# Band stage of layer 0: scores issued two units ahead and next to the values, with minima and exponentials reordered to match

## What is computed

```python
s = jnp.einsum('bcqhd,bckhd->bchqk', qc, kb).astype(F32) * (HD_A ** -0.5)
s = s + rel_bias_lookup(table, dist)
p = jax.nn.softmax(s, axis=-1).astype(v.dtype)
o = jnp.einsum('bchqk,bckhd->bcqhd', p, vb)
...
y = jnp.concatenate([mix_o, cross_attn(xq, mk, mv)], axis=-1) * jax.nn.silu(gate)
return x + y @ w
```

## Time and profile before

| what | value |
|---|---|
| median of 3 runs | 2691.19 us (2688.42 to 2704.43) |
| span of the profiled execution | 2696.0 us |
| TensorE busy | 2554.8 us, 95% |
| VectorE busy | 1918.9 us, 71% |
| ScalarE busy | 1457.8 us, 54% |
| GpSimd busy | 353.8 us, 13% |
| band stage in the trace | about 700 to 1415 us |

### The profile page before, as it was taken

How to read it: one execution, slowest core, us unless ns; L and a number is a source line. 1 busy time by engine, 2 the same in 40 slices (tenths; PEclk the granted TensorE clock), 3 DMA queues, 4 the chain that set the end, 5 groups by cost and what they waited for, 6 DMA issues and landing times. The chain is left out here.

```text
span 2696.0 us, 53797 instructions
## 1 busy us (share of the span) xinstructions
PE 2554.8 (95%) x19893; PEld 2252.6 (84%) x19893; DVE 1918.9 (71%) x3676; ACT 1457.8 (54%) x3352; POOL 353.8 (13%) x581
## 2 busy tenths in 40 slices
PE   6999999999789999999997999999999799999997
PEld 3999999999556777777777989999999688888886
DVE  5899787877345555555558998787886777777774
ACT  3555666655235554554545656667665555555553
POOL 1332000000012111111112320000001011111111
PEclk9999999999759999999998999999999899999998
DMA  4888887788573221221235887777787823333331
GB/s 169 279 289 260 277 273 240 232 280 261 137 218 87 73 87 58 73 87 58 85 122 198 283 280 243 243 246 243 243 285 235 244 83 99 99 99 99 105 99 53
DMA packets 402535, 480.13 MB, mean 178 GB/s; under 512 B 40516, under 2 KB 249212, under 8 KB 402280
## 3 DMA queue, kind: packets, MB, share of 16 engines
q1 hardware_dynamic: 385592, 416.51, 49.3%
q0 software_dynamic: 14848, 55.45, 6.0%
q10 hardware_dynamic: 1840, 4.75, 0.6%
HBM read 329.78 MB, written 151.56 MB: 179 GB/s over the span
## 5 line engine op out<-in xcount | busy, mean ns | idle before, releaser
L1354 PE MATMUL pj_acc<-x_hi,pj_wh 128*128 128x256 f32 (+1 forms) x3136 | 920.8, 294 | 33.8 <-DVE pj_wl L461 31.1
L1354 PE MATMUL pj_acc<-x_lo,pj_wh 128*128 128x256 f32 (+1 forms) x3136 | 908.5, 290 | 0.0
L1354 PE MATMUL pj_acc<-x_hi,pj_wl 128*128 128x256 f32 (+1 forms) x3136 | 908.4, 290 | 0.0
L454 ACT ACTIVATE pj_wh<-pj_wt 128x512 fp32r<-128x512 f32 x728 | 456.6, 634 | 359.5 <-DMA pj_wt<-tsum 262.7
L1354 PEld LDWEIGHTS pj_acc<-x_hi,pj_wh 128*128 128x128 f32 x3136 | 599.5, 191 | 48.9 <-DVE pj_wl L461 46.3
L1354 PEld LDWEIGHTS pj_acc<-x_hi,pj_wl 128*128 128x128 f32 x3136 | 599.9, 191 | 0.0
L1354 PEld LDWEIGHTS pj_acc<-x_lo,pj_wh 128*128 128x128 f32 x3136 | 599.3, 191 | 0.0
L461 DVE SCALAR_TENSOR_TENSOR pj_wl<-pj_wt,pj_wh 128x512 fp32r<-128x512 f32 x728 | 507.7, 712 | 111.0 <-ACT pj_wh L454 99.4
L1205 DVE TENSOR_TENSOR pj_out<-pj_out,pj_acc 128x512 f32<-128x512 f32 (+1 forms) x448 | 320.0, 714 | 91.8 <-PE pj_acc L1354 59.3
L2448 ACT COPY pb_pt<-pb_TP 128x384 f32<-128x384 f32 (+2 forms) x272 | 107.3, 395 | 325.3 <-PE pb_TP L2178 244.8
L2339 DVE COPY pb_pt<-pb_TP 128x256 f32<-128x256 f32 (+2 forms) x266 | 115.8, 436 | 145.9 <-PE pb_TP L2175 133.6
(11 more groups left out here) (312 smaller groups left out, 4078.8 us busy)
## 6 DMA issues: line engine op xcount, KB each, us to landing
pj_wt<-tsum SPq DMA_DIRECT2D x588, 256.0 KB, 3.5
proj<-pj_out SPq DMA_DIRECT2D x112, 512.0 KB, 4.2
tsum<-pj_wt SPq DMA_DIRECT2D x140, 256.0 KB, 3.3
pj_wraw<-in_w_in_dram POOLq DMA_DIRECT2D x24, 1024.0 KB, 6.3
tsum<-pj_wraw SPq DMA_DIRECT2D x56, 256.0 KB, 4.1
hg_x<-x_mid SPq DMA_DIRECT2D x17, 512.0 KB, 3.5
out_dram<-hg_x POOLq DMA_DIRECT2D x17, 512.0 KB, 3.0
pb_gate<-proj SPq DMA_DIRECT2D x16, 512.0 KB, 5.0
```

The costliest lines, as they stand in the source:

```text
L454: nc.scalar.mul(self.hi[j][:], self.source(step), scale_of(c, self.l)).then_inc(self.s_hi, 1)
L1354: ins = nc.tensor.matmul(BANK[j][:, 0:n], a[j][:, k], x.of(y, p, j)[:, k], start=(k == 0 and i == 0), stop=(k == 3 and i == 2))
```

## The change

It moves instructions only; none is added or removed, and no tile changes its size.

- TensorE, prompt tiles: four products instead of two stand between `turn(u, 0)` and `turn(u, 1)` (three at p = 6); `scores` is issued for u + 2 instead of u + 1, after `turn(u, 1)`, directly ahead of `values(u)`; the products that are left (two; none at p = 3 and 7, where they go ahead of the scores; three at p = 6) follow `values(u)`. `turn_values` follows `values` at p = 6.
- VectorE: `low_min(u+1, 1)` before `high(u, 1)`, `low_min(u+2, 0)` after it. ScalarE: `exp(u+1, 1)` and `exp(u+2, 0)` close a unit.
- The two cross units write their scores at columns 0 and 512 of `SC[h]`, in two banks, so that the second need not wait for the first one's exponentials.
- The sample tile (T = 0) keeps its order; its last unit also issues the scores, a minimum and an exponential of u + 2.

```diff
+        def cross_of(p):
+            return slice(512 * (p - MG), 512 * (p - MG) + NMEM)
...
-                    if is_cross(*step(u - 1)):
+                    if is_cross(*step(u - 1)) and not is_cross(T, p):
                         pe.wait_ge(s_exp, 2 * u)
...
+                for u in range(PAIRS, U_ALL):
                     T, p = step(u)
+                    mid = 6 if p % 4 == 3 else 3 if p == MG else 4
                     turn(u, 0)
+                    project(T - 1, 6 * p, 6 * p + min(mid, 4))
                     turn(u, 1)
+                    project(T - 1, 6 * p + min(mid, 4), 6 * p + mid)
+                    if u + 2 < U_ALL:
+                        scores(u + 2)
+                    values(u)
                     if p == MG and T < NT:
                         turn_values(T + 1)
-                    values(u)
+                    project(T - 1, 6 * p + mid, 6 * p + 6)
...
+                for u in range(PAIRS, U_ALL):
                     T, p = step(u)
                     high(u, 0)
                     inverse(u)
                     if u + 1 < U_ALL:
                         low_min(u + 1, 1)
+                    high(u, 1)
+                    if p % 4 == 0:
+                        low_part(T - 1 if p == 0 else T, 1 - p // 4)
                     if p % 4 == 3:
+                        add(T - 1, p // 4)
+                    if u + 2 < U_ALL:
+                        low_min(u + 2, 0)
+                    if p % 4 == 3:
                         dve.wait_ge(s_pv, u + 1)
                         dve.wait_ge(s_gr, u + 1)
                         gate(T, p // 4)
...
+                for u in range(PAIRS, U_ALL):
                     T, p = step(u)
                     low(u, 0)
+                    if p % 4 == 0:
                         y_high(T - 1 if p == 0 else T, 1 - p // 4)
+                    if p == MG:
+                        exp(u + 1, 1)
                     low(u, 1)
+                    if p != MG and u + 1 < U_ALL:
+                        exp(u + 1, 1)
                     if p == MG and T < NT:
                         values_low(T + 1)
+                    if u + 2 < U_ALL:
+                        exp(u + 2, 0)
```

More of the change, by code:

```diff
@@ L2137, in scores @@
                             po = HD * h
-                            nc.tensor.matmul(SC[h][:, 0:NMEM], xq[T % 2][po:po + HD, p - MG],
+                            nc.tensor.matmul(SC[h][:, cross_of(p)], xq[T % 2][po:po + HD, p - MG],
                                              mem_kT[po:po + HD, l, p - MG], start=True, stop=True).then_inc(s_sc, 1)
@@ L2282, in _ @@
                 turn_keys(0, 0)
-                for u in range(U_ALL):
+                for u in range(PAIRS):
+                    turn(u, 0)
+                    if u + 1 < PAIRS:
+                        keys_turn(u + 1)
+                    scores(u + 1)
+                    turn(u, 1)
+                    if u == MG:
+                        turn_values(1)
+                    if u == PAIRS - 1:
+                        scores(u + 2)
+                    values(u)
+                for u in range(PAIRS, U_ALL):
                     T, p = step(u)
+                    mid = 6 if p % 4 == 3 else 3 if p == MG else 4
                     turn(u, 0)
[L2286 to L2291, removed]
+                    project(T - 1, 6 * p, 6 * p + min(mid, 4))
                     turn(u, 1)
-                    if T:
-                        project(T - 1, 6 * p + 2, 6 * p + 6)
+                    project(T - 1, 6 * p + min(mid, 4), 6 * p + mid)
+                    if u + 2 < U_ALL:
+                        scores(u + 2)
+                    values(u)
                     if p == MG and T < NT:
                         turn_values(T + 1)
-                    values(u)
+                    project(T - 1, 6 * p + mid, 6 * p + 6)
                 for i in range(4):
@@ L2309, in low_min @@
                     if is_cross(T, p):
-                        nc.vector.tensor_reduce(mn[:, at:at + 1], SC[h][:, 0:NMEM], AX_X, ALU.min).then_inc(s_min, 1)
+                        nc.vector.tensor_reduce(mn[:, at:at + 1], SC[h][:, cross_of(p)], AX_X, ALU.min).then_inc(s_min, 1)
                         return
@@ L2393, in _ @@
                 keys_out_high(0, tT[:].rearrange("p g n -> p (g n)"))
-                for u in range(U_ALL):
+                for u in range(PAIRS):
+                    high(u, 0)
+                    inverse(u)
+                    if u + 1 < PAIRS:
+                        keys_high(u + 1)
+                    if u == 4:
+                        low_part(0, 0)
+                    low_min(u + 1, 0)
+                    high(u, 1)
+                    low_min(u + 1, 1)
+                    for k in chunks(u):
+                        weights_low(k)
+                    if u == PAIRS - 1:
+                        low_min(u + 2, 0)
+                    if u % 4 == 3:
+                        dve.wait_ge(s_pv, u + 1)
+                        dve.wait_ge(s_gr, u + 1)
+                        gate(0, u // 4)
+                    if u == MG:
+                        values_high(1)
+                for u in range(PAIRS, U_ALL):
                     T, p = step(u)
@@ L2397, in _ @@
                     inverse(u)
[L2398 to L2404, removed]
                     if u + 1 < U_ALL:
                         low_min(u + 1, 1)
-                    if T == 0:
-                        for k in chunks(p):
-                            weights_low(k)
+                    high(u, 1)
+                    if p % 4 == 0:
+                        low_part(T - 1 if p == 0 else T, 1 - p // 4)
                     if p % 4 == 3:
-                        if T:
-                            add(T - 1, p // 4)
+                        add(T - 1, p // 4)
+                    if u + 2 < U_ALL:
+                        low_min(u + 2, 0)
+                    if p % 4 == 3:
                         dve.wait_ge(s_pv, u + 1)
@@ L2439, in exp @@
                     n = tiles_of(T, p) * P
-                    src = SC[h] if is_cross(T, p) else se[u % 2][h]
-                    nc.scalar.activation(se[u % 2][h][:, 0:n], src[:, 0:n], ACT.Exp, bias=mn[:, at:at + 1], scale=-1.0,
+                    src = SC[h][:, cross_of(p)] if is_cross(T, p) else se[u % 2][h][:, 0:n]
+                    nc.scalar.activation(se[u % 2][h][:, 0:n], src, ACT.Exp, bias=mn[:, at:at + 1], scale=-1.0,
                                          accum_out=tot[:, at:at + 1]).then_inc(s_exp, 1)
@@ L2484, in _ @@
                 exp(0, 1)
-                for u in range(U_ALL):
+                for u in range(PAIRS):
+                    low(u, 0)
+                    if u + 1 < PAIRS:
+                        keys_low(u + 1)
+                    if u == 4:
+                        y_high(0, 0)
+                    low(u, 1)
+                    exp(u + 1, 0)
+                    if u == MG:
+                        values_low(1)
+                    exp(u + 1, 1)
+                    for k in chunks(u):
+                        weights_high(k)
+                    if u == PAIRS - 1:
+                        exp(u + 2, 0)
+                for u in range(PAIRS, U_ALL):
                     T, p = step(u)
                     low(u, 0)
-                    if T == 0 and p + 1 < PAIRS:
-                        keys_low(p + 1)
-                    if p % 4 == 0 and u:
+                    if p % 4 == 0:
                         y_high(T - 1 if p == 0 else T, 1 - p // 4)
+                    if p == MG:
+                        exp(u + 1, 1)
                     low(u, 1)
-                    if u + 1 < U_ALL:
-                        exp(u + 1, 0)
+                    if p != MG and u + 1 < U_ALL:
+                        exp(u + 1, 1)
                     if p == MG and T < NT:
                         values_low(T + 1)
[L2497 to L2501, removed]
+                    if u + 2 < U_ALL:
+                        exp(u + 2, 0)
                 y_high(NT, 1)
```

## The result

| | before | after |
|---|---|---|
| median | 2692.45 us (2687.54 to 2704.83, 6 runs) | 2713.05 us (2710.35 to 2720.72, 6 runs) |
| ratio to before | | 1.0081, interval 1.0053 to 1.0109 |
| profiled span | 2696.0 us | 2711.4 us |

A forecast was written before the change was run, and what follows sets the result against it. TensorE's order was taken to bound the prompt tiles. A full tile summed to +1.9 us (shape gain -0.87, waits more), all tiles to +26, taken as +25: median 2716 us, own range 2708 to 2724, overall range 2697 to 2731.

The forecast's parts named there:

- The bound: Prompt tiles: TensorE, busy 609.8 of 615 us, sets the time; every microsecond it gains or loses goes into the total.
- One change of shape less: Band units: three changes of array shape instead of four, gaining 0.87 us per tile, 14 us over 16 prompt tiles.
- that rival: Scores to values free: no array stand between the two half shapes, 19 us off, total 2697; chance 0.12.
- its bounds of 0 and 0.3: Direct change from 64x128 to 128x64: taken as 0.15 us, between free and two ordinary changes; 19 us either way.
- The chain: First transposes, copy, reciprocal, GpSimd `rb` copy, second transposes: 1.74 us in five-tile units, so TensorE stands 0.27 us.
- The cover of 1.47: Between first and second transposes: the transposes and four products fill 1.47 us, against 2.45 us before.
- The rest of the tile: Full tile: shape gain of 0.87 against waits at the other units and p = 1 to 5, summing to +1.9 us.
- the wait for the copies of the next values: Before p = 7: a wait of 0.21 us already there moves and grows by 0.1 us at most.
- The total: All prompt tiles: +26 us summed, taken as +25, giving a median of 2716 us.
- Costs nothing: Separate cross banks, moved minima and exponentials, unmoved transfers, sample tile: no cost beyond named waits; sample tile 0, bounds -1 and +1.
- The banks: Separate banks of the cross scores: remove a wait not in the rows before, so put at nothing.
- ScalarE falls behind: From p = 4, `turn(u, 1)` waits for a late copy out of `TP`: 0.9 us more per tile, total 2730; chance 0.20.

The follow-up runs named there:

- e6: Changed kernel with one more GpSimd copy of the same size ahead of the one writing `rb`, prompt tiles; 2737.8 us, ratio to before 1.0163.
- e9: Changed kernel, reciprocal before the copy out of `TP`, products spread (6 at p = 0 to 4, 4 at 5 and 7, 5 + 5 at 6); 2670.6 us, ratio 0.9935.
- e1: Changed kernel with the reciprocal ahead of the first copy out of `TP` in VectorE's queue, prompt tiles only; 2693.6 us, ratio to before 1.0004.
- e3: Changed kernel with six products between the two groups of transposes (three at p = 6), reciprocal left in place; 2681.3 us, ratio to before 0.9961.
- e5: Changed kernel with the two products that follow the values moved between scores and values (p = 0, 1, 2, 4, 5); 2721.0 us, ratio to before 1.0100.
- e2: Kernel before with the reciprocal ahead of the first copy out of `TP` in VectorE's queue; 2689.0 us, ratio to before 0.9994.
- e7: Kernel before with one more GpSimd copy ahead of the one writing `rb`, prompt tiles; 2699.8 us, ratio to before 1.0022.
- e8: Changed kernel with both cross units at column 0 of `SC` and the wait for the exponentials back; 2737.9 us, ratio to before 1.0163.

## Why the prediction held, point by point

- **The bound.** TensorE's order sets the prompt tiles: what an edit does to their stretch shows in the total, within some 6 us (+21.0 and +20.6 for the change, +47 and +44 for e6, -20 and -17 for e9).
- **One change of shape less.** Predicted 0.64 us of changes a unit against 0.55, or 0.50 without a product behind the values. A unit without its wait is 5.35 in e1 and 5.27 in e3, against 5.42 before: 0.07 and 0.15 gained where 0.09 and 0.14 were forecast, so this is right. e5 shows the direct change at the ordinary price, so that rival is gone, and its bounds of 0 and 0.3 too.
- **The chain.** Predicted 1.74 us from load to load, a return of 0.08, 0.27 lost, a band unit of 5.58. Measured: return 0.07, unit 5.57, the array idle for 0.23. The cover of 1.47 was right (1139.15 to 1140.62). The chain came out 0.04 shorter: in the rows above the copy starts 0.75 after the first transpose and not 0.81, the return is 0.01 shorter, and the second transposes start 0.03 after their load, 1.70 in all. That the reciprocal's place behind the copy is the cause, e1, e3, e6 and their counterparts on the kernel before (e2, e7) show together.
- **The rest of the tile.** Predicted +1.9 a tile, measured +1.5 (42.05 against 40.54). This is the step that was mis-sized. From the loads and products of the changed kernel, the array stands 0.39 at p = 0 (said 0.5), 0.32 and 0.08 at p = 6 and 7 (0.36 and 0.13), 0.13 ahead of the next tile's scores (0.25), 0.25 ahead of the values at p = 4 and 5 (0.3), and 1.15 at p = 1 to 5 (1.35); the wait for the copies of the next values grows by 0.02 (0.1). Each term had its place right and was put 0.04 to 0.2 us too long, at p = 1 to 5 by the 0.04 a unit of the point above. That all the others erred the same way may be because I let each wait start from an undisturbed unit; no run shows it. The terms as measured add up to 0.2 us a tile less than the tile lost, and that I can't assign, so part of my excess was made up for by something that I don't have.
- **The total.** +26, taken as +25, measured +21 on the stretch and +20.6 in the medians. The excess is the 0.4 us in each of eleven full tiles, and 1.4 in tiles 1 to 4: tile 1 gained 0.4 (said 0), tiles 2 to 4 lost 3.0 (said 4); the last tile lost 0.2 more than said. A tile of 42.05 is also just below the 42.2 to 42.5 that I named as a sign.
- **Costs nothing.** The sample tile: see below, it moves by more than my bound of 1, in either direction and in unchanged code. The banks: e8.
- **ScalarE falls behind.** Real at p = 0 alone, where the array still stands 0.39 us in e1 although `rb` is early there. In the other band units it keeps its distance even in e3 and e9, where no product follows the values.

## What to carry to other kernels

An instruction that fills TensorE between a producer and the wait on its result is part of that wait's cover: before moving it, follow the chain that runs meanwhile through all engines, add its returns, and compare it with what is left in between. Here the repair was free, since the late link (a reciprocal whose input had been ready for 2.8 us) only stood behind a copy in its queue. Waits of some 0.2 us behind a product didn't show in the list of matmul waits; compare starts. And filling work is best kept where something waits: the same 48 products a tile gave 628 or 599 us with the reciprocal in its place, and 609, 597 or 587 with it moved.

## What the hardware showed that was not expected

The sample tile takes very different times, although no edit of an experiment touches it (the change itself only adds a group of scores, a minimum and an exponential to its last unit). From its first transpose of `rb` to that of the first prompt unit it is 76 us in the profile of before, 68 in that of after, and 61 to 78 in the others; before, e2 and e7, which have the same instructions there, take 76, 61 and 68. Stretches of that part, before and then after (length, busy times, granted clock, DMA share, GB/s):

```profile
718.00:794.00 76.00, 57.90 (x585) 42.98 (x584) 30.36 (x74) 28.39 (x65) 6.74 (x17) 0.57 0.73 228
```

```profile
722.00:790.00 68.00, 50.17 (x585) 38.01 (x584) 29.74 (x76) 28.56 (x67) 6.70 (x17) 0.70 0.81 254
```

The same matmuls ran at a mean granted clock of 0.57 and 0.70, that is with more or less of the stretch at the 1.2 GHz level, and TensorE was busy for 58 and 50 us. The two ends of the eleven profiles say the same: 61 us at 0.86 in e2, 78 at 0.54 in e8. TensorE stands again and again there for copies by ScalarE and VectorE; in the prompt tiles, where it hardly does, the clock is 1.00 in both. This is a spread of up to 17 us that no edit of the prompt tiles causes, and it is why I read small effects from the stretch. Whether the clock sets that time or only goes with it, these runs don't settle.
